# Weight splits in quarters, pooled tiles kept in PSUM, top-k rounds spread out, in a fused two-block layer kernel

## What is computed

```python
for i in range(2):                                    # first block
    x = layer_norm(ALPHA*x + 0.5*swiglu(x, ffn1[i]))  # D_FF = 2816
    m = pool_mixer(x) if i == 0 else dilated_attention(x)
    x = layer_norm(ALPHA*x + m)
    x = layer_norm(ALPHA*x + 0.5*swiglu(x, ffn2[i]))
for l in range(2):                                    # second block
    h = rms_norm(x)*(1+scale) + shift                 # modulation: silu(c) @ ada_w
    p = split(h @ w_in[l])
    y = sig(g0)*(retention @ w0) + sig(g1)*(sparse_attention @ w1) + sig(g2)*(gla @ w2)
    x = x + gate * rms_norm(y @ w_out[l])

def pool_mixer(x):      # four groups of 256 channels, windows 2, 4, 8, 16
    u = x @ w_in
    mixed = mean_of_centred_window(u) - u             # at the ends fewer tokens count
    return ((mixed @ w_group) * scale) @ w_out
```

## Time and profile before

| | |
|---|---|
| median of three runs | 3788.59 us |
| the profiled execution: its time, its span | 3787.25 us, 3785.4 us |
| TensorE (PE) busy | 3440.3 us, 91% of the span |
| GpSimd (POOL) busy | 2200.1 us, 58% |
| VectorE (DVE) busy | 1737.8 us, 46% |
| ScalarE (ACT) busy | 798.0 us, 21% |
| mean granted clock of TensorE | 0.955 |

### The profile page before, as it was taken

One profiled execution on the slowest core, in us unless ns is written; L12 is line 12 of the kernel. 1 busy time (PEld: TensorE's weight loads), 2 busy tenths in 40 slices (PEclk: granted clock), 3 DMA queues, 4 the chain that ended last, 5 costly groups with the idle time before them and its releaser, 6 DMA issues.

```text
span 3785.4 us, 42681 instructions
## 1 busy us (share of the span) xinstructions
PE 3440.3 (91%) x16956; PEld 2739.8 (72%) x16956; DVE 1737.8 (46%) x2017; ACT 798.0 (21%) x1345; POOL 2200.1 (58%) x558
## 2 busy tenths in 40 slices
PE   6999878999899979989897999868999987899997
PEld 5887656888688858778775888646678765667875
DVE  6772574222422242351536222365667525566742
ACT  1000212110211022231323110031322212132321
POOL 6776555777577746436353777635445663445564
PEclk9999989999899989999998999979999998999998
DMA  5553222323223222112121232212222221222221
GB/s 179 177 177 107 82 67 67 96 90 98 72 89 98 92 78 89 45 56 81 42 78 45 78 100 95 89 55 67 62 63 66 77 91 56 62 56 67 68 81 64
DMA packets 321300, 312.56 MB, mean 83 GB/s; under 512 B 11376, under 2 KB 303888, under 8 KB 320784
## 3 DMA queue, kind: packets, MB, share of 16 engines
q1 hardware_dynamic: 303840, 277.91, 23.7%
q10 hardware_dynamic: 17328, 32.80, 2.5%
HBM read 308.57 MB, written 2.10 MB: 82 GB/s over the span
## 4 chain that ended last, share of the span: by engine, by line
PE 74%; DVE 15%; ACT 5%; issue 4%; DMA 2%; ACTq 0%; DVEq 0%
PE ps L358 48%; PE ps L1229 12%; PE ps L989 4%; DVE sq L1110 2%; PE ps L1271 2%; PE ps L463 1%; DMA ada_raw<-in_ada_w 1%; ACT x L494 1%; PE ps L1796 1%; ACT xh L500 1%; DVE at_sc L912 1%; DVE score L1561 1%; DVE top L1560 1%; DVE d_pr L1650 1%; PE ps L1609 1%
## 5 line engine op out<-in xcount | busy, mean ns | idle before, releaser
L337 POOL TENSOR_TENSOR wh<-w_raw,zero 128x2048 fp32r<-128x2048 f32 (+2 forms) x277 | 952.4, 3438 | 1522.1 <-PE ps L358 1016.0
L339 POOL TENSOR_TENSOR wl<-w_raw,wh 128x2048 fp32r<-128x2048 f32 (+2 forms) x277 | 1247.6, 4504 | 21.7
L358 PE MATMUL ps<-xh,wh 128*128 128x512 f32 x2160 | 857.1, 397 | 101.7 <-DVE xl L536 48.0
L358 PE MATMUL ps<-xl,wh 128*128 128x512 f32 x2160 | 847.9, 393 | 0.0
L358 PE MATMUL ps<-xh,wl 128*128 128x512 f32 x2160 | 847.5, 392 | 0.0
L358 PEld LDWEIGHTS ps<-xh,wh 128*128 128x128 f32 x2160 | 409.3, 190 | 211.0 <-issue 91.9
L358 PEld LDWEIGHTS ps<-xh,wl 128*128 128x128 f32 x2160 | 409.7, 190 | 86.7
L358 PEld LDWEIGHTS ps<-xl,wh 128*128 128x128 f32 x2160 | 410.3, 190 | 83.0 <-issue 1.0
L1229 PE MATMUL ps<-xh,wh 128*128 128x512 f32 x688 | 294.0, 427 | 8.1 <-ACT stats L1371 6.4
L358 PE MATMUL ps<-hid_h,wh 128*128 128x512 f32 x704 | 279.7, 397 | 7.6 <-DVE mod L1125 7.6
L626 DVE TENSOR_TENSOR hp<-sg,ps 128x512 f32<-128x512 f32 x88 | 60.3, 685 | 481.2 <-PE ps L358 481.2
(11 more groups left out here) (286 smaller groups left out, 5102.0 us busy)
## 6 DMA issues: line engine op xcount, KB each, us to landing
w_raw<-in_w_in SPq DMA_DIRECT2D x120, 512.0 KB, 4.1
w_raw<-in_ffn_w_gate SPq DMA_DIRECT2D x88, 512.0 KB, 4.6
w_raw<-in_ffn_w_up SPq DMA_DIRECT2D x88, 512.0 KB, 4.8
w_raw<-in_attn_w_qkv SPq DMA_DIRECT2D x72, 512.0 KB, 4.5
w_raw<-in_ffn_w_down SPq DMA_DIRECT2D x64, 512.0 KB, 3.6
ada_raw<-in_ada_w ACTq DMA_DIRECT2D x24, 512.0 KB, 5.5
stats<-in_ada_w ACTq DMA_DIRECT2D x24, 512.0 KB, 5.1
w_raw<-in_ffn_w_down SPq DMA_DIRECT2D x32, 384.0 KB, 4.1
```

The costliest lines, as they stand in the source:

```text
L337: t = s["w_hi"].up(pool.tensor_tensor(hi, raw, self.zero[:, 0:1].to_broadcast([P, n]), ALU.subtract))
L339: s["w_lo"].up(pool.tensor_tensor(lo, raw, hi.bitcast(F32), ALU.subtract))
L358: mm = self.nc.tensor.matmul(out, a[:, slot, w], b(t), start=start and t == 0 and q == 0, stop=stop and t == k - 1 and q == 2)
```

## The change

There are three parts.

1. POOL splits a chunk in quarters. It issues high 0, high 1, low 0, high 2, low 1, high 3, low 2, low 3, eight instructions in place of two. Each low one waits for the high one of its quarter. TensorE is still told only at the end, after low 3.
2. In the pool stage all four groups have PSUM banks of their own, so TensorE no longer waits for the copies of earlier groups. The copy to `padded` stays, but the mixed value, the product with the group matrix and its scaled form stay in the same PSUM tiles. The mean is a multiplication by a constant within one instruction (scalar_tensor_tensor) after the two ends of 8 tokens have been multiplied by a small table `edges`. The scaling of early groups is put between the mixing of later ones, in ACT's and in DVE's program.
3. In the mixer, eight of the sixteen rounds of block 1 go into the index loop (two after each of the pairs 2 to 5). The sixteen rounds of block 2 are two in each of the eight retention steps; none stand ahead of the first.

```diff
 def pool_weights(self, pool):
-            t = s["w_hi"].up(pool.tensor_tensor(hi, raw, self.zero[:, 0:1].to_broadcast([P, n]), ALU.subtract))
-            pool.wait_ge(s["w_hi"].sem, t)
-            s["w_lo"].up(pool.tensor_tensor(lo, raw, hi.bitcast(F32), ALU.subtract))
+            parts = [slice(q * n // 4, (q + 1) * n // 4) for q in range(4)]
+            zero, done = self.zero[:, 0:1].to_broadcast([P, n // 4]), []
+            def high(q):
+                done.append(s["w_hi"].up(pool.tensor_tensor(hi[:, parts[q]], raw[:, parts[q]], zero, ALU.subtract)))
+            def low(q):
+                pool.wait_ge(s["w_hi"].sem, done[q])
+                return pool.tensor_tensor(lo[:, parts[q]], raw[:, parts[q]], hi[:, parts[q]].bitcast(F32), ALU.subtract)
+            high(0)
+            for q in range(1, 4):
+                high(q)
+                low(q - 1)
+            s["w_lo"].up(low(3))
 def pe_pool(self, pe, st):
-                if g >= 2:
-                    pe.wait_ge(s["u_ready"].sem, st.at("u_ready", 2 * g + m - 3))
-                self.product(pe, c % 2, KT, 256, m * P, ps[:, 2 * (g % 2) + m], self.x_parts(),
+                self.product(pe, c % 2, KT, 256, m * P, ps[:, 2 * j + m], self.x_parts(),
 def act_pool(self, act, st):
+        move(0); move(1); high(0); move(2); high(1); move(3)
+        scale(0); high(2); scale(1); high(3); scale(2); scale(3)
 def dve_pool(self, dve, st):
+            for e, at in enumerate((PAD, T)):
+                edge = src[:, :, at:at + PAD]
+                self.dve_then(dve, nc.vector.tensor_tensor(edge, edge, self.edges[:, g, e].unsqueeze(1).to_broadcast([P, 2, PAD]), ALU.mult))
             for m in range(2):
-                mix = self.mix[:, g % 2, m]
-                self.dve_then(dve, nc.vector.tensor_tensor(mix, src[:, m, PAD:PAD + T], self.inv_count[:, g], ALU.mult))
-                s["mixed"].up(nc.vector.tensor_tensor(mix, mix, u[:, m, PAD:PAD + T], ALU.subtract))
+                u = ps[:, 2 * j + m]
+                s["mixed"].up(nc.vector.scalar_tensor_tensor(u, src[:, m, PAD:PAD + T], 0.5 ** (g + 1), u, ALU.mult, ALU.subtract))
+        for j in range(GROUPS):
+            windows(j)
+            low(j)
+            if j >= 2:
+                scaled_low(j - 2)
+        scaled_low(2)
+        scaled_low(3)
 def dve_mixer(self, dve, st):
         for u in range(INDEX_PAIRS):
             self.dve_index_pair(dve, st, u)
+            if u >= 2:
+                self.dve_choose_rounds(dve, 1, 2)
-        self.dve_choose_rounds(dve, 1, TOPK // 8)
+        self.dve_choose_rounds(dve, 1, TOPK // 16)
         self.dve_choose_biases(dve, 1)
-        self.dve_choose_rounds(dve, 2, TOPK // 16)
...
-            if i >= 4:
-                self.dve_choose_rounds(dve, 2, TOPK // 64)
+            self.dve_choose_rounds(dve, 2, TOPK // 64)
```

More of the change, by code:

```diff
@@ L154 @@
             x_ready=KT, xh_ready=KT, acts=KT)
+POOL_ORDER = (0, 1, 2, 3)
+POOL_TILES = tuple(2 * g + m for g in POOL_ORDER for m in range(2))
 POOLED = dict(u_ready=KT, mixed=KT, mixed_hi=KT, mixed_lo=KT, y_full=KT, y_hi=KT, y_lo=KT, z_ready=KT)
@@ L313, in each_chunk @@
                 n = len(loads)
-                with rolled(eng, count, {self.s[k]: n for k in raised}) as i:
+                with rolled(eng, count, {self.s[k]: n * per for k, per in raised.items()}) as i:
                     for q, load in enumerate(loads):
@@ L348, in wait_chunk, with product @@
         pe.wait_ge(self.s["w_lo"].sem, PRIMED["w_lo"] + c + 1)
-    def product(self, pe, slot, k, width, c0, out, xs, start=True, stop=True, before=None, count=True, t0=0):
+    def product(self, pe, slot, k, width, c0, out, xs, start=True, stop=True, before=None, count=True, t0=0, order=None):
         xh, xl = xs
-        for t in range(k):
+        order = order or range(k)
+        for t in order:
             if before:
@@ L357, in product @@
             for q, (a, b) in enumerate(((self.wh, xh), (self.wh, xl), (self.wl, xh))):
-                mm = self.nc.tensor.matmul(out, a[:, slot, w], b(t), start=start and t == 0 and q == 0,
-                                           stop=stop and t == k - 1 and q == 2)
+                mm = self.nc.tensor.matmul(out, a[:, slot, w], b(t), start=start and t == order[0] and q == 0,
+                                           stop=stop and t == order[-1] and q == 2)
         if count:
@@ L663, in out_chunks, with pe_out @@
         return (2, [self.halves(w, 0, KT, (256 * mp, 512), 256) for mp in range(2)])
-    def pe_out(self, pe, st, c1, xs, before=None):
+    def pe_out(self, pe, st, c1, xs, before=None, order=range(KT)):
         with rolled(pe, 2, {self.s["acc"]: 4}) as i:
@@ L743, in act_pool @@
-        for n in range(KT):
-            self.wait_group(act, st, n // 2)
-            if n >= 2:
-                act.wait_ge(s["y_lo"].sem, st.at("y_lo", n - 1))
-            t = s["y_full"].up(nc.scalar.activation(self.y[:, n % 2], ps[:, 4 + n % 4], ACT.Copy, scale=self.pool_scale[:, n:n + 1]))
-            act.wait_ge(s["y_full"].sem, t)
-            s["y_hi"].up(nc.scalar.activation(self.y_h[:, n], self.y[:, n % 2], ACT.Copy))
+                act.wait_ge(s["acc"].sem, self.acc(st.chunk0 + j, m))
@@ new lines, in move, with high, scale @@
+                if j >= 2:
+                    act.wait_ge(s["mixed"].sem, st.at("mixed", 2 * j - 2))
+                s["u_ready"].up(nc.scalar.activation(self.padded[:, j % 2, m, PAD:PAD + T], ps[:, 2 * j + m], ACT.Copy))
+        def high(j):
+            for m in range(2):
+                act.wait_ge(s["mixed"].sem, st.at("mixed", 2 * j + m + 1))
+                s["mixed_hi"].up(nc.scalar.activation(self.y_h[:, POOL_TILES[2 * j + m]], ps[:, 2 * j + m], ACT.Copy))
+        def scale(j):
+            self.wait_group(act, st, j)
+            for m in range(2):
+                n, y = POOL_TILES[2 * j + m], ps[:, 2 * j + m]
+                t = s["y_full"].up(nc.scalar.activation(y, y, ACT.Copy, scale=self.pool_scale[:, n:n + 1]))
+                act.wait_ge(s["y_full"].sem, t)
+                s["y_hi"].up(nc.scalar.activation(self.y_h[:, n], y, ACT.Copy))
@@ L750, in act_pool @@
+        move(0)
+        move(1)
+        high(0)
+        move(2)
+        high(1)
+        move(3)
+        scale(0)
+        high(2)
+        scale(1)
+        high(3)
+        scale(2)
+        scale(3)
         self.act_norm(act, st, self.ln_of("pool", 0), 0)
```

82 lines of the change are left out of this document (37 added, 45 removed).

## The result

| kernel | median us | range of the runs | profiled span | mean granted clock |
|---|---|---|---|---|
| before | 3788.95 | 3788.31 to 3789.50 | 3785.4 | 0.955 |
| changed | 3691.34 | 3690.43 to 3699.67 | 3690.3 | 0.968 |

The account below looks back on a forecast made before the run. TensorE, busy 91%, bounds the kernel; gains must come from its idle 345 us, mostly waits on DVE. Terms sum to 70, less 4 in ffn 0 and 2 for POOL stalls: 64, so 3725 us; range 3700 to 3765.

Parts of the forecast that it names:

- ffn 0, charged with 4: Eleven rounds of ffn 0: bursts of modulation instructions hold POOL up; a loss of 4 us, between 0 and 35.
- Price on POOL, 9.5 us a chunk: POOL's full weight chunk grows from 8.3 us to 9.5, six extra instructions costing 1.1 us plus seams.
- The first rival: POOL instructions over 512 elements cost more than the line says; at 0.5 each, 3865 us; chance 0.08.
- The mixers' small ones, 11: Mixers: most of the 6 us on L1650 (`d_pr`) and a like amount of small waits go; 11 us, bounds 4 and 16.
- Attention, 11: Once per attention quad, L935 waits less for POOL, 0.5 of it from the clock; four times 2.8, 11 us.
- Norms, 7: Six norms: L438 ends 2.4 us earlier but pair sums meet POOL; net 1.2 each, 7 us, bounds 0 and 14.
- Pool stage, 15: Pool stage: output projection starts at 514 in place of 529 after one late chain; 15 us, bounds 9 and 19.
- Retention, 19.4: Both mixers: moving top-k rounds from ahead of `st_a` removes TensorE's 9.7 us stop in each; 19.4 us, bounds 16 and 21.
- No wait on `st_a`: Sign that the prediction is right: TensorE no longer waits for `st_a` in the mixers, where it stopped 9.7 us each.
- Less 2 for stalls of POOL: Outside ffn 0, small POOL stalls cost 2 us, deducted from the sum of gains.
- The port doesn't change hands: Rival: no handover between POOL's quarters, or many short DVE waits; quarters bring nothing or cost 4; about 3757; chance 0.08.
- More goes than I count: Rival: TensorE's waits that name SBUF operations go nearly whole, at 90 us; 3698 us; chance 0.05.

Follow-up runs that it names:

- no_idx_rounds: Changed kernel with eight top-k rounds of block 1 moved back from the index loop to ahead of the retention; 3696.41 us.
- v1_order: Changed kernel with another pool-stage order: ScalarE makes group 2's high parts before scaling group 0, DVE all windows before any scaled low part; 3695.78 us.
- part 1 alone: Kernel before with only POOL's weight split in quarters, eight instructions a chunk; 3718.77 us.
- whole ones: Changed kernel with the quarter split undone, so POOL uses two instructions a chunk and the pool-stage and top-k changes stay; 3747.30 us.
- eighths: Changed kernel with sixteen POOL instructions a chunk, 256 elements each, in place of eight; 3757.10 us.
- the angles alone: Changed kernel with the first mixer's second table of rotation angles, and ScalarE's sines of it, moved into the index loop; 3681.63 us.

## Why the prediction missed

**The step that failed is the price of a removed wait.** The prediction says that "a gain must come out of its idle 345 us": the sum took each wait at its length and let the clock give back something in one place only, the attention stage, 0.5 four times. Of the 31 us that are missing (95.1 against 64), 21.4 are this in the profiled execution: TensorE was busy 23.4 us less, and I had charged 2. The second quad of the attention stage shows it, before first (from its first stop of 2.75 us on), then changed:

```profile
1650.80:1656.00 5.20, 1.97 (x8) 0.50 0.00 0
1656.00:1666.00 10.00, 10.00 (x96) 0.78 0.33 107
```
```profile
1610.40:1616.00 5.60, 4.44 (x50) 1.00 0.01 3
1616.00:1626.00 10.00, 7.49 (x78) 1.00 0.33 105
```

Two stops of 2.75 and 3.23 us put the clock at 0.50 (1.2 of 2.4 GHz) for 5.2 us and at a mean of 0.78 for the next ten. With stops of 1.19, 0.67 and 0.68 it stays at 1.00. The quad idles 1.8 us less and is busy 2.4 less. Windows of before show the low clock behind its waits; I read the waits and not these windows.

Short stops do not always keep the clock up. The same quad in no_idx_rounds begins with the same two stops, 1.19 and 0.68 us:

```profile
1617.30:1622.90 5.60, 4.71 (x30) 0.70 0.01 3
1622.90:1632.90 10.00, 8.46 (x96) 1.00 0.33 105
```

There the quad idles 3.4 us less than in before and is busy 0.2 more, 3.2 in all against 4.2 in the changed kernel. Both are above the 2.8 of the prediction, and in such an execution the clock is not the reason: the idle terms are. So the failed step has two parts that hold in either execution: the clock's share was charged with 2 and is 8 to 23, and the terms for ffn 0 (-4, measured 2.7 and 2.8) and for the mixers' small waits (11, measured 20.6 and 20.6) were too small. How far the time falls below 3700 is in part chance: the eight executions of the changed kernel have a median of 3694.3, and the two slowest took 3699.7 and 3701.3.

**The other 9.7 us are idle time** in the profiled execution, 61.9 forecast and 71.6 measured, term by term:
- *ffn 0, charged with 4, "but they come in bursts"*: the use of POOL's room was right, the conclusion not. I had forecast 2.4 + 2.8 = 5.2 of 6.2 us per round; the timeline of POOL in the changed kernel has 0.36 + 0.54 left, so 5.3 were used. But TensorE lost nothing: I take it that a burst is levelled out between the two chunks that are on their way, which no run tested by itself. The rounds even gained 0.3 us each. The error is 5.2 of idle time. Two chunks of POOL in such a round:

```profile
153.01 2.53 POOL L344 TENSOR_TENSOR wh<-w_raw,zero 128x512 fp32r<-128x512 f32 x2 [0.36 <-PE ps L373]
155.51 1.74 POOL L348 TENSOR_TENSOR wl<-w_raw,wh 128x512 fp32r<-128x512 f32 x1
157.21 1.03 POOL L344 TENSOR_TENSOR wh<-w_raw,zero 128x512 fp32r<-128x512 f32 x1
158.21 1.29 POOL L348 TENSOR_TENSOR wl<-w_raw,wh 128x512 fp32r<-128x512 f32 x1
...
163.99 2.04 POOL L344 TENSOR_TENSOR wh<-w_raw,zero 128x512 fp32r<-128x512 f32 x2 [0.54 <-PE ps L373]
```

- *Price on POOL, 9.5 us a chunk*: from start to start an undisturbed high and low take 1.00 and 1.25, four pairs 9.0 us, against 8.27 in the earlier trace rows. So 0.12 for an extra instruction, not 0.18 and seams of 0.08: one starts before the other has ended. The first rival (instructions over 512 cost more) is out. DVE's hold on POOL was sized too low: 0.45 (1.29 to 1.74) in place of 0.2 to 0.35. Both errors cancel in ffn 0. The Trainium skill (SBUF — State Buffer, "Who interferes with whom") has the one that comes second blocked for the whole instruction of the first; for POOL behind DVE it is 0.45 of 0.69 us, and in this the measurement decides.
- *The mixers' small ones, 11*: 13.6 of idle time (13.3 with part 1 alone), and 7.1 of clock on top. The bound of 16 was below 20.6. The 6.0 on `d_pr` went as forecast; the "like amount of small ones" was larger. These waits of before are gone, all but 0.6 us on `gx`:

```profile
PE ps L1229 <- DVE mx_y L1435: 3.7, 2, 1.8
PE ps L1796 <- DVE gx L1852: 3.4, 4, 1.4
PE ps L1527 <- DVE ik L2153: 2.3, 1, 2.3
```

- *Attention, 11*: idle time 11.0, of which I had charged 9; clock 6.3 in place of 2. At the lower clock (no_idx_rounds) it is 14.4 in all.
- *Norms, 7*: 8.0. The gap before the mean fell from 4.3 to 1.7. In the first three norms both pair sums met POOL, as charged: they take 1.29 and 1.56 us in place of 0.68 twice, the gap before the sum of the squares grew from 3.2 to 3.8, and a stop of 0.6 stands behind it. That leaves 1.4 to 1.6 of the 2.56, near the 1.2 of the prediction.
- *Start, 2.5, end of ffn 0's rounds, 4*: 1.9 and 4.4 of idle time.
- *Pool stage, 15*: 14.9 of idle time. The projection starts at 496.79 after a gap of 6.5, and what is late is the chain that I named, down to `high` and `scale` of ScalarE ahead of the last windows; v1_order shows that most of its length is POOL's and not the order's.
- *Retention, 19.4*: 16.6 of idle time. "No wait on `st_a`" was wrong: 1.4 us of each 9.7 are the decay product itself (1.23) and its hand-over, which nobody moved. The clock gave 4.6, so the total hid the error; that the sum of this term came out right to 1.8 us is luck.
- *Less 2 for stalls of POOL*: three new waits on `wl`, 0.4, 0.8 and 1.0 us, so 2.2. They lie in the pool stage and in a mixer and are in the sums of these.

Of what was to show the mechanism, nearly all came: 2216 tensor instructions on POOL, quarters of 1.04 and 1.29, few waits on `wl`, the norm's addition at 1.19, the wait on `y_l` 19.9 to 8.1, a higher clock. *The port doesn't change hands* is refuted by the four lines of the norm's addition above. *More goes than I count*, 3698 at a chance of 0.05, came nearest; its reason, that the SBUF waits go nearly whole, is not what happened.

What stays open: why in one execution the clock falls after a given stop and in the next it doesn't. The runs show that it happens, and what it costs.

## What to carry to other kernels

When a wait of TensorE is removed, take its length and then read the granted clock in the ten microseconds behind it: here 71.6 us of idle time brought 23.4 more in one execution, about 78 brought 8 to 10 in two at a lower clock, and stops that were put in cost two thirds to three quarters on top. Compare the sum of both in a stretch before its parts. Where DVE waits for the end of another engine's instruction, cut that instruction as long as its engine keeps idle time in its tightest stage: quarters left 0.9 us a round and won 56 us over whole ones, eighths lost 66 again. Of a chain that is moved, only as much counts as the wait is long, so look for the next chain instead of moving more: the angles alone were worth 10.

## What the hardware showed unexpectedly

- A DVE instruction with two SBUF inputs stretches POOL's piece by 0.45 us, a high one as a low one (1.04 to 1.49, 1.29 to 1.74). This is paid at every seam that lets DVE in, so more pieces mean more loss on POOL: a chunk of eight took 12.65 us beside a DVE that never paused.
- Even a DVE product over 16 elements waits for the end of POOL's piece: two took 2.11 us in place of 0.38.
- The mean granted clock of the same program varied between 0.963 and 0.968 from one execution to the next, and its time by 11 us with it, while the kernel before stayed within 2 us in the same series, and within 5 in another (0.954 to 0.956 in both).
- The same two stops, 1.19 and 0.68 us, were followed by a granted clock of 1.00 in one kernel and 0.70 in a kernel whose TensorE program is the same. In the attention stage the slower TensorE then waited less, so that most of the loss did not show in the time.
